# First half of x on ScalarE's queue, identity products on TensorE at the start, turned chunks in pairs

## The reference

```
h = rmsnorm(x, g_mix);  z = h @ w_in                     # 2048 x 12800
q_r, f_r, i_r, og_r, q_a, k_a, v_a, gate_a, gate_b = split(z)
o_a = gated linear recurrence(q_r, f_r, i_r, og_r), 16 heads, chunks of 64
o_b = banded attention(q_a, k_a, v_a, sinks), 32 heads, rotary: cos and sin of
      positions * THETA ** (-i / 32)
x = x + concat(sigmoid(gate_a) * o_a, sigmoid(gate_b) * o_b) @ w_out
x = x + square(relu(rmsnorm(x, g_mlp) @ w_up)) @ w_down  # 2048 -> 8192 -> 2048
x = x + sigmoid(x @ w_ple_gate) * (p @ w_ple_proj)
return rmsnorm(x, g_final)
```

## Time and profile before

| | |
|---|---|
| median of 3 runs | 1716.85 us (1716.4 to 1717.51) |
| the profiled execution | 1718.0 us |
| its span | 1716.3 us |
| TensorE busy | 1696.1 us, 99% of the span |
| VectorE, ScalarE, GpSimd busy | 1102.8, 925.0, 16.9 us |
| DMA | 315.30 MB, mean 184 GB/s |
| mean granted TensorE clock | 0.998 |

### The profile page before, as it was taken

How to read it: one execution, slowest core, us unless ns; L and a number is a source line. 1 busy time by engine, 2 the same in 40 slices (tenths; PEclk the granted TensorE clock), 3 DMA queues, 4 the chain that set the end, 5 groups by cost and what they waited for, 6 DMA issues and landing times.

```text
span 1716.3 us, 22351 instructions
## 1 busy us (share of the span) xinstructions
PE 1696.1 (99%) x8669; PEld 1416.6 (83%) x8669; DVE 1102.8 (64%) x1405; ACT 925.0 (54%) x1227; POOL 16.9 (1%) x72
## 2 busy tenths in 40 slices
PE   7999999999999999999999999999999999999997
PEld 6888888788887888878888888888888888888886
DVE  6667866875668756687585565656555556566565
ACT  6466647655565555655546554544444445454454
POOL 3000000000000000000000000000000000000000
PEclk9999999999999999999999999999999999999999
DMA  6655555556655566555556666666666665655554
GB/s 216 203 174 180 173 173 168 176 176 181 185 180 173 173 183 185 173 173 176 181 177 212 186 192 191 190 190 193 190 193 188 194 189 193 190 190 187 181 184 136
DMA packets 163292, 315.30 MB, mean 184 GB/s; under 512 B 10161, under 2 KB 10482, under 8 KB 163058
## 3 DMA queue, kind: packets, MB, share of 16 engines
q1 hardware_dynamic: 162016, 312.01, 59.5%
q10 hardware_dynamic: 1170, 1.87, 0.3%
HBM read 311.74 MB, written 2.10 MB: 183 GB/s over the span
## 4 chain that ended last, share of the span: by engine, by line
PE 98%; DVE 1%; ACT 1%; DMA 0%; issue 0%; SPq 0%; DVEq 0%; ACTq 0%
PE acc L678 22%; PE acc L679 22%; PE acc L684 22%; PE acc L692 6%; PE turn L692 6%; PE turn L678 3%; PE turn L679 3%; PE turn L684 3%; PE turn L698 3%; PE acc L698 3%; PE turn L720 2%; PE turn L747 0%; PE turn L771 0%; PE turn L820 0%; PE turn L759 0%; DMA w_raw<-in_w_in_dram 0%
## 5 line engine op out<-in xcount | busy, mean ns | idle before, releaser
L1334 DVE TENSOR_TENSOR w_lo<-w_raw,w_hi 128x1024 fp32r<-128x1024 f32 x588 | 720.0, 1224 | 562.9 <-ACT w_hi L977 560.2
L977 ACT ACTIVATE w_hi<-w_raw 128x1024 fp32r<-128x1024 f32 x588 | 622.7, 1059 | 700.7 <-PE acc L684 444.9
L678 PE MATMUL acc<-w_hi,hT 128*128 128x512 f32 x1104 | 435.6, 395 | 4.4 <-ACT w_hi L977 4.4
L679 PE MATMUL acc<-w_hi,hT 128*128 128x512 f32 x1104 | 431.1, 390 | 0.0
L684 PE MATMUL acc<-w_lo,hT 128*128 128x512 f32 x1104 | 296.2, 390 | 0.0
L678 PEld LDWEIGHTS acc<-w_hi,hT 128*128 128x128 f32 x1104 | 207.8, 188 | 48.4 <-ACT w_hi L977 5.6
L684 PEld LDWEIGHTS acc<-w_lo,hT 128*128 128x128 f32 x1104 | 207.8, 188 | 43.6
L679 PEld LDWEIGHTS acc<-w_hi,hT 128*128 128x128 f32 x1104 | 208.0, 188 | 41.9
L678 PE MATMUL acc<-w_hi,mT_hi 128*128 128x512 f32 x416 | 164.4, 395 | 0.0
L679 PE MATMUL acc<-w_hi,mT_lo 128*128 128x512 f32 x416 | 162.2, 390 | 0.0
L692 PE MATMUL acc<-hT,w_hi 128*128 128x512 f32 x448 | 140.0, 394 | 0.0
(11 more groups left out here) (247 smaller groups left out, 1545.7 us busy)
## 6 DMA issues: line engine op xcount, KB each, us to landing
w_raw<-in_w_in_dram SPq DMA_DIRECT2D x232, 512.0 KB, 3.7
w_raw<-in_w_up_dram SPq DMA_DIRECT2D x128, 512.0 KB, 3.8
w_raw<-in_w_down_dram SPq DMA_DIRECT2D x128, 512.0 KB, 4.3
w_raw<-in_w_out_dram SPq DMA_DIRECT2D x64, 512.0 KB, 3.8
w_raw<-in_w_ple_gate_dram SPq DMA_DIRECT2D x32, 512.0 KB, 4.6
x_sb<-in_x_dram SPq DMA_DIRECT2D x8, 256.0 KB, 7.4
w_raw<-in_w_ple_proj_dram SPq DMA_DIRECT2D x4, 512.0 KB, 3.7
out_dram<-x_sb SPq DMA_DIRECT2D x6, 256.0 KB, 3.1
```

The costliest lines, as they stand in the source:

```text
L678: pe.matmul(a, hi[:, k, t, :], w_hi[:, s, kk, :], start=first and kk == 0, stop=False)
L679: pe.matmul(a, lo[:, k, t, :], w_hi[:, s, kk, :], start=False, stop=False)
L977: act.activation(w_hi[:, n % W_SLOTS], w_raw[:, n % RAW_SLOTS], ACT.Copy)\
L1334: dve.tensor_tensor(w_lo[:, n % W_SLOTS], w_raw[:, n % RAW_SLOTS], w_hi[:, n % W_SLOTS].bitcast(F32), ALU.subtract).then_inc(w_lo_ready, 1)
```

## The change

The first half of x (quarters 0 and 1) is issued by ScalarE instead of SyncE. `posi` and `sink_bc` move from ScalarE's queue to SyncE's, behind x quarter 3. TensorE gets 6 + 2 + 5 products of the identity with itself, around the turn of the rows and after the first turns of x; their result is never read. In slot 0 VectorE runs `x_lo` before `split_lo`. Turned chunks run in pairs: the high products of both, then the low products of both.

```diff
-            load_x(0)
             for slot in HEAD:
                 load(slot)
-                if slot[0] in (1, 2, 3):
+                if slot[0] in (2, 3):
                     load_x(slot[0])
+                if slot[0] == 3:
+                    with nc.allow_non_contiguous_dma(reason="256 positions"):
+                        sp.dma_start(posi[:], positions[0].rearrange("(t p) -> p t", p=P)).then_inc(pos_landed, 16)
+                    sp.dma_start(sink_bc[:], sinks[0].partition_broadcast(P)).then_inc(sinks_landed, 16)
...
+                if turned(kind, j):
+                    if c % 2:
+                        turned_pair(n - 1, col, c - 1, last, r)
+                    return
                 s = n % W_SLOTS
                 pe.wait_ge(w_hi_ready, count(n + 1, r, LOOP_CHUNKS))
-                if turned(kind, j):
-                    turned_chunk(n, col, c, s, first, last, r)
-                    return
...
+            def turned_pair(n, col, c, last, r):
+
+                for c_, s in ((c, n % W_SLOTS), (c + 1, (n + 1) % W_SLOTS)):
+                    pe.wait_ge(w_hi_ready, count(n + 1 + c_ - c, r, LOOP_CHUNKS))
+                    for kk in range(2):
+                        for ct in range(4):
+                            pe.matmul(turned_acc(col, ct)[:], w_hi[:, s, kk, ct * P:(ct + 1) * P],
+                                      hT[:, 2 * c_ + kk].rearrange("p a t c -> p (a t c)"),
+                                      start=c_ == 0 and kk == 0, stop=False)
+                for c_, s in ((c, n % W_SLOTS), (c + 1, (n + 1) % W_SLOTS)):
+                    pe.wait_ge(w_lo_ready, count(n + 1 + c_ - c, r, LOOP_CHUNKS))
+                    for kk in range(2):
+                        for ct in range(4):
+                            mm = pe.matmul(turned_acc(col, ct)[:, 0:TT * P], w_lo[:, s, kk, ct * P:(ct + 1) * P],
+                                           hT_hi[:, 2 * c_ + kk].rearrange("p t c -> p (t c)"), start=False,
+                                           stop=last and c_ > c and kk == 1)
+                    mm.then_inc(w_used, 1)
...
+            def idle_products(n):
+
+                for _ in range(n):
+                    pe.matmul(acc[1][1][:, 0:P], ident[:], ident[:], start=True, stop=True)
...
             pe.wait_ge(ident_made, 1)
+            idle_products(6)
             pe.wait_ge(rows_landed, 16 * 4)
             pe.transpose(bank(("rows",))[:, 0:P], rows[:], ident[:]).then_inc(full(("rows",)), 1)
+            idle_products(2)
...
                             x_turn("xT", cb, t)
+                if n == 0:
+                    idle_products(5)
                 chunk(slot)
...
             act.dma_start(rows[64:65, :], hgrn_norm_g).then_inc(rows_landed, 16)
-            with nc.allow_non_contiguous_dma(reason="256 positions"):
-                act.dma_start(posi[:], positions[0].rearrange("(t p) -> p t", p=P)).then_inc(pos_landed, 16)
-            act.dma_start(sink_bc[:], sinks[0].partition_broadcast(P)).then_inc(sinks_landed, 16)
+            for cb in range(2):
+                cs = slice(cb * COLS, (cb + 1) * COLS)
+                for t in range(TT):
+                    act.dma_start(x_sb[:, t, cs], x[0, t * P:(t + 1) * P, cs]).then_inc(x_landed[t][cb], 16)
             nc.scalar.preload_act_table_set("trig_and_small")
...
                         x_weighted(0, slot[0] // 2, t)
+                if slot[0] == 0:
+                    for t in range(TT):
+                        x_lo(0, 0, t)
                 split_lo(slot)
-                if slot[0] in (0, 2, 4, 6):
+                if slot[0] in (2, 4, 6):
                     for t in range(TT):
                         x_lo(0, slot[0] // 2, t)
```

## The result

The changed kernel took 1722.15 us (median of 8 runs, 1721.33 to 1722.78); the kernel before took 1716.88 (8 runs, 1716.4 to 1717.96). The ratio is 1.003, 95% interval [1.0019, 1.0041]: 5.3 us slower. The profiled execution took 1722.28, its span is 1720.5.

What follows compares the result with a forecast made beforehand. TensorE, 99% busy, was taken to bound the kernel. Late angles 3.9 plus clock 1.1 less pairs 1.2 gave +3.8 on 1718.0, so 1721.8, less 1.15: 1720.7 us; forecast's own range 1718.3 to 1722.9, overall range 1715.8 to 1723.6.

Steps and rivals of the forecast that it cites:

- The deciding wait: ScalarE waiting at the sines for GpSimd's angles: positions land at 15.8, angles ready at 32.5, chunk 6 starts at 37.3 us.
- GpSimd's stretch: GpSimd's chain of angles, slowed beside VectorE's four `split_lo` and two pairs of `x_lo`: 4.7 us on top of 12.0.
- The clock term: TensorE's clock falling to the low level over the idle stretch before chunk 6: 1.1 us, between 0 and 2.2.
- Chunk 8: Start of chunk 8 on TensorE: 3.9 us later through the late angles, plus 1.1 us for the clock.
- Pairs: Turned chunks (w_up groups 1 to 7): 56 pairs save 0.02 us each, 1.2 us gained, bounds 0 and 1.7.
- Taking 1.15 us off for the profiled execution: The profiled execution of the kernel before lay 1.15 us over the runs' median, so 1.15 came off the sum.
- The front: Stretch before chunk 0: it starts 1.3 us earlier, 0.9 by VectorE's order and 0.4 by x on ScalarE's queue.
- VectorE's new order: Slot 0, `x_lo` no longer behind the first `split_lo`: first `hT_lo` ready 0.9 us earlier.

## Why the prediction was right, point by point

**The deciding wait: right.** Cast at 15.97 (15.8 taken), angles at 31.92 (32.5), ScalarE standing 7.5 us (6 to 9), TensorE 4.3 us (3 to 6), chunk 6 at 36.8 (37.3). Three runs hold it from three sides: the issue moved back takes 6.2 us away, the move alone (with `sink_bc`) adds 7.6, and the wait put two chunks later takes 6.8 away with the positions as late as ever.

**GpSimd's stretch: right to 1 us.** 4.7 us were entered for four `split_lo` and two pairs of `x_lo`; the chain is 15.95 - 12.0 = 4.0 us longer than unhindered.

**The clock term: mis-sized.** 1.1 us was taken between 0 and 2.2. The clock did fall, in every product of chunk 6. In the trace it cost 1.8 us (chunk 8 at 44.72 against 42.94 with TensorE kept busy), or 2.1 counted from the start of chunk 6 (7.93 against 5.87 us); in the medians 1.3.

**Chunk 8: right in the sum.** 3.9 + 1.1 = 5.0 expected, 5.4 in the trace: 3.6 with the clock kept up (42.94 - 39.32) and 1.8 for the clock.

**Pairs: right.** 1.2 expected (56 x 0.02 is 1.1), 1.1 in the traces and 1.15 in the medians of the run by itself, whose interval holds no gain too.

**Taking 1.15 us off for the profiled execution: wrong.** The profiled execution of before lay 1.1 us over its median (1718.0 to 1716.88), that of the changed kernel only 0.1 over (1722.28 to 1722.15). The distance is no constant that passes to another kernel. From profile to profile the change is 4.3 us, 3.8 were forecast; from median to median it is 5.3. Most of the 1.45 us that the forecast was short is this. The one other kernel with the old front unchanged, the pairs alone, shows the same: its profiled execution is 0.96 over its median (1717.03 to 1716.07), and its clock steps up near 17.8 us as well. That the old front meets this step at differing times from run to run would explain it; no profile of a faster execution of it exists, so this stays open.

**The front: wrong in the parts, hidden in the sum.** Chunk 0 was to start 1.3 us earlier and started at 11.98. x was later (turns at 7.10 and 9.08 instead of 5.33 and 6.49): beside it the weights came earlier (`w_hi` of chunk 0 at 7.39 instead of 8.83), which nobody needs so early. The prediction asked only when the weights land, not when x does. The sum held because the wait at chunk 6 covers whatever the front does. There was luck in it too: TensorE was done with chunk 5 about 1.5 us earlier than before (1.3 foreseen), yet not from an earlier start but from the clock, which stepped up at 14.5 instead of 17.8 and was entered as 0. And an identity product costs two records of 0.21 us at the low clock, 0.43 us, not the 0.21 of a transpose: the five took 2.1 us and held chunk 0 back a little. The first `hT_lo` was ready at 10.84 + 0.69 = 11.53; where TensorE stood idle chunk 0 followed 0.15 us behind it, here 0.45:

```profile
10.84 1.47 DVE L1390 TENSOR_TENSOR hT<-tmp,hT 128x512 fp32r<-128x512 f32 x2
```

Taken out, the products were worth 0.9 us in the medians with x late (cause not shown) and 2.0 us with x early (the clock).

**VectorE's new order: start oversized, worth undersized.** 0.9 us was entered for the start of chunk 0. In the front with x on SyncE it gave 0.6 there, and 1.9 in the medians, the rest by the clock. In the changed kernel, with x late, it wasn't tested by itself.

## What to carry to other kernels

When a DMA changes places, follow its consumer to the end: the place of a 1 KB transfer was worth 6.2 us here (7.6 together with `sink_bc`), since a chain of 28 operations on GpSimd hung on it and ScalarE waited in program order for that chain. Put a wait on a side chain behind what the critical engine needs next, and issue a small input early if a long chain hangs on it, but not in the queue of bulk that is needed first. Splitting the bulk over two queues added no bandwidth once the engines were full: 392 GB/s from 6.5 to 15.5 us before and after; it brought the weights earlier and x, needed first, later. The best version measured has the pairs, VectorE's order and the identity products, with x and the positions issued as in the kernel before and only `sink_bc` late: 1712.8 us.

## What the runs showed of the hardware

- TensorE's clock fell to 1.2 GHz over an idle stretch of 4.29 us (granted 0.85, then 0.50), and over one of 5.45; where identity products filled the stretch it stayed up (granted 1.00 from 33 to 44 us).
- For the low level at the start of the kernel before, the granted clock reads 1.00 (12.0 to 17.5 us) while products are 0.43 us apart. The spacing is the surer reading there.
- The positions (256 words of 4 bytes) at the start of ScalarE's queue did not delay the first weights: `w_hi` of chunk 0 at 7.99 to 8.13 us with them, 7.94 and 8.04 without. With `sink_bc` beside them it was 8.83 and 9.11.
- With x in ScalarE's queue, the positions ahead of it by 0.45 us of issue made the turns of x begin 1.6 and 1.4 us later (8.66 and 10.43 against 7.10 and 9.08).
- An identity product of 128 x 128 in float32 left two records and took 0.43 us at the low clock and 0.23 at the high one (24 of them in 5.5 us).
